# Last two down pairs in column parts of 308 and 220 with their weights kept on chip, and the last sums ahead of the spreads

## The chip, the core and the metric

The kernel runs on one NeuronCore of a Trainium2 chip. The metric is the device time of one execution in microseconds. The core has TensorE (matrix products into PSUM), VectorE, ScalarE, GpSimd and SyncE, which here only issues DMAs. The profile calls them PE (with PEld for the loading of weights), DVE, ACT, POOL and SP. All data is float32 in DRAM. Each engine runs its instructions in order, and semaphores are the only tie between engines.

## The reference

One layer of a decoder with three parallel token mixers, a gated merge, then a SwiGLU feed-forward and a final RMSNorm. The change touches the last part alone:

```python
h2 = rmsnorm(x, norm2_w)
gu = h2 @ w_ffn_up
x = x + ((silu(gu[..., :D_FF]) * gu[..., D_FF:]) @ w_ffn_down)
...
def rmsnorm(x, w):            # final norm, with final_norm_w
    return x * rsqrt(mean(x * x, axis=-1) + EPS) * w
```

with D_MODEL 1024, D_FF 2816 and 1056 tokens (1024 of the prompt, 32 of the samples). The outputs of the step are `y` for all tokens and the new states of the mixers.

## The kernel before, in words

The tensors lie with channels in the 128 partitions and the T = 1056 tokens along the free dimension. X1 holds the residual in 8 tiles of 128 channels (KD = 8). Each float32 operand of a large product is split into a high part (rounded to fp32r) and a low part, and a product is three matmuls (high weight by low data, low weight by high data, high by high), lines 2229 to 2231.

The feed-forward is done in *pairs*, each a 2 by 2 block product in Strassen's way: seven products, numbered 1 to 7, whose results are added to the four quadrants (two channel tiles by two halves of the 528 tokens). Pairs 0 to 19 are the up projection, pairs 20 to 35 (PAIRS = 36) the down projection: four groups of depth, with four pairs of output tiles in each. Pair 32 + m of the last group makes channel tiles 2m and 2m + 1 final, so pair 34 finishes tiles 4 and 5, pair 35 tiles 6 and 7. In this group a product is deep 3 tiles, so it is 3 x 3 matmuls for a *chunk* of columns. Each product covers 528 columns in two chunks of 264 (c = 0 and 1), in two PSUM banks (`quad`); one product is 18 matmuls.

**Weights.** For each product ScalarE casts the weight to its high part (`weight_high`, line 2762), and GpSimd subtracts to get the low part (`low`). Products 5, 7, 6 and 4 need a difference of raw weights first, made by GpSimd in place (`difference`). The order on GpSimd for a pair is: low of the first product, two differences, two lows, a difference, a low, a difference, three lows; all have line 1305. The parts go into a ring of six slots (`ring`), in WH, WL and RINGB. Slot g is free once product g - 6 is done, and ScalarE issues the cast of product g four products ahead (AHEAD). TensorE waits for the low part (`wl_ok`) ahead of each product. Raw weights are loaded two pairs ahead into RAWB (even pairs) and WRAW (odd pairs).

**Order of products.** Pairs take 1, 5, 7, 6, 2, 3, 4 (ORDER); the last pair takes 1, 5, 7, 6, 4, 3, 2 (LAST_ORDER) and is made chunk by chunk from its second product on: product 1 whole, six products for c = 0, six for c = 1. VectorE adds each result to X1 (`down_add`, `last_down_add`, line 2927), nine adds for a pair or a chunk of it, and product 6 enters three quadrants. A product may overwrite its bank only when the add of the bank's last product is done (semaphore `dd`).

**Final norm.** ScalarE squares each finished tile (into SQ5 and GT), VectorE adds the squares into AC5. Tiles 0 to 5 are added over all 1056 columns at once. Tiles 6 and 7 are done for four *groups* of 264 columns: group g is the upper half for g even, the lower for g odd, chunk g // 2. For a group TensorE sums AC5 over the partitions in three blocks of 88 tokens (`final_sums`, line 2259), ScalarE takes the root, VectorE the reciprocal, TensorE spreads it over the partitions (`final_spread`, line 2267), ScalarE copies it from PSUM (`spread_copy`). Then GpSimd scales tiles 0 to 2 and VectorE tiles 3 to 7 (`final_rows`, line 2935), and three DMAs store the group (tiles 0 to 2, 3 to 5, 6 and 7), all by SyncE but for the first of group 3, which ScalarE issues. Sums and spreads of groups 0 and 1 stand between products of the last chunk; those of groups 2 and 3 follow the last product as sums 2, spread 2, sums 3, spread 3. The order on each engine is written out by hand.

## Times and profile before

| | us |
|---|---|
| median of 3 executions | 1685.45 |
| lowest and highest | 1684.84, 1686.82 |
| profiled execution, its own time | 1684.72 |
| its span | 1683.0 |
| TensorE busy | 1653.4 (98%) |
| VectorE, ScalarE, GpSimd busy | 965.2, 556.0, 791.2 |

The span runs from the first instruction to the last of the profiled execution; the time of that execution is 1.7 us more. A matmul's busy time is longer than its distance to the next, since they are pipelined: its cost in a stream is the distance between starts. Times in the rows count from the start of the span. A row of the view in order of time has start, duration (of all that it merges), engine, line, operation, names written and read, shapes, how many, and in brackets the engine's idle time before it and what ended that. GpSimd and VectorE rows give the duration of a single instruction only where x1 stands.

### The profile page before, as it was taken

The numbers are of one execution on the slowest core, as the hardware profiler recorded it, in microseconds if no ns is written. First come the engines' busy times: TensorE is split into PE (matmuls) and PEld (weight loads), VectorE is DVE, ScalarE is ACT, GpSimd is POOL, SyncE is SP. The second block draws the span as 40 slices with busy tenths as digits, with TensorE's granted clock in tenths as the row PEclk, the third lists the DMA queues.
The fourth block names the chain that finished last, engine by engine and source line by source line (L and its number), as shares of the span: only waits on it lengthen the run. The fifth ranks groups of instructions, "written<-read, shape, count | busy, mean of one in ns | idle before, by whom it ended". The sixth has DMA issues, their size and how long they took to land. (4 is left out here: it accounts for less than half of the span.)

```text
span 1683.0 us, 30880 instructions
## 1 busy us (share of the span) xinstructions
PE 1653.4 (98%) x12241; PEld 1604.5 (95%) x12241; DVE 965.2 (57%) x1642; ACT 556.0 (33%) x1240; POOL 791.2 (47%) x756
## 2 busy tenths in 40 slices
PE   7999999999999999999999999999999999999997
PEld 7999999999999998889899999999999999999997
...
## 3 DMA queue, kind: packets, MB, share of 16 engines
...
q14 instruction: 42, 0.34, 0.1%
...
## 5 line engine op out<-in xcount | busy, mean ns | idle before, releaser
L1636 PE MATMUL ps<-HL,WH 128*128 128x384 f32 (+1 forms) x1536 | 507.3, 330 | 4.3 <-DVE HL L689 1.8
L1637 PE MATMUL ps<-HH,WL 128*128 128x384 f32 (+1 forms) x1536 | 496.9, 324 | 0.0
L1638 PE MATMUL ps<-HH,WH 128*128 128x384 f32 (+1 forms) x1536 | 496.1, 323 | 0.0
L1636 PEld LDWEIGHTS ps<-HL,WH 128*128 128x128 f32 x1536 | 289.2, 188 | 15.5 <-issue 9.4
L1637 PEld LDWEIGHTS ps<-HH,WL 128*128 128x128 f32 x1536 | 289.4, 188 | 0.3
L1638 PEld LDWEIGHTS ps<-HH,WH 128*128 128x128 f32 x1536 | 289.2, 188 | 0.0
L1280 POOL TENSOR_TENSOR WL<-WRAW,WH 128x1024 fp32r<-128x1024 f32 x59 | 145.6, 2467 | 246.9 <-DMA WH<-in_w 246.9
L1277 POOL DMA_DIRECT2D WH<-in_w x59 | 34.5, 585 | 348.6 <-PE ps L1638 347.1
L2927 DVE TENSOR_TENSOR X<-X,ps 128x528 f32<-128x528 f32 (+2 forms) x170 | 107.8, 655 | 155.3 <-PE ps L2231 104.4
L2320 ACT ACTIVATE GT<-ps 128x384 f32<-128x384 f32 (+1 forms) x72 | 33.3, 464 | 214.7 <-PE ps L1638 177.5
L2927 DVE TENSOR_TENSOR RB<-RB,ps 128x528 f32<-128x528 f32 x60 | 42.1, 701 | 103.5 <-ACT RB L2842 86.0
L1305 POOL TENSOR_TENSOR WRAW<-WRAW 128x512 f32<-128x512 f32 (+2 forms) x72 | 92.0, 1278 | 9.9 <-DVE STG L2927 4.6
L1305 POOL TENSOR_TENSOR RAWB<-RAWB 128x512 f32<-128x512 f32 (+2 forms) x72 | 87.5, 1215 | 5.4
L2229 PE MATMUL ps<-HL,RINGB 128*128 128x264 f32 x272 | 77.5, 285 | 2.1 <-DVE GT L2927 2.1
L2230 PE MATMUL ps<-HH,RINGB 128*128 128x264 f32 x280 | 79.5, 284 | 0.0
L2231 PE MATMUL ps<-HH,RINGB 128*128 128x264 f32 x280 | 79.5, 284 | 0.0
L2229 PE MATMUL ps<-HL,WH 128*128 128x264 f32 x274 | 78.0, 285 | 0.4 <-issue 0.4
L2229 PE MATMUL ps<-HL,WL 128*128 128x264 f32 x270 | 76.6, 284 | 0.0
L2229 PE MATMUL ps<-SOP,RINGB 128*128 128x264 f32 x264 | 75.2, 285 | 0.0
L2230 PE MATMUL ps<-HH,WL 128*128 128x264 f32 x264 | 75.0, 284 | 0.0
L2231 PE MATMUL ps<-SOP,RINGB 128*128 128x264 f32 x264 | 75.0, 284 | 0.0
L2230 PE MATMUL ps<-SOP,RINGB 128*128 128x264 f32 x264 | 74.9, 284 | 0.0
...
## 6 DMA issues: line engine op xcount, KB each, us to landing
...
```

Source lines behind the costliest of these rows:

```text
L1277: nc.gpsimd.dma_start(WH[:, slot, 0:wd], src[:, 0:wd]).then_inc(s_high[slot], 16)
L1280: nc.gpsimd.tensor_tensor(WL[:, slot, 0:wd], WRAW[:, slot, 0:wd], WH[:, slot, 0:wd].bitcast(F32), ALU.subtract).then_inc(split_ok, 1)
L1305: return nc.gpsimd.tensor_tensor(out, a, b, op)
L1636: nc.tensor.matmul(out, wh, rl, start=start, stop=False)
L1637: nc.tensor.matmul(out, wl, rh, start=False, stop=False)
L1638: return nc.tensor.matmul(out, wh, rh, start=False, stop=stop)
L2229: nc.tensor.matmul(out, wh, ml, start=product in FRESH and k == 0, stop=False, skip_group_check=True)
L2230: nc.tensor.matmul(out, wl, mh, start=False, stop=False, skip_group_check=True)
L2231: last = nc.tensor.matmul(out, wh, mh, start=False, stop=k == nk - 1, skip_group_check=True)
L2320: nc.scalar.activation(GT[:, c0:c0 + w], acc_of(no, n)[:, 0:w], ACT.Tanh, scale=0.5).then_inc(acc_free[n], 1)
L2927: return nc.vector.tensor_tensor(out, a, b, op)
```

## The change

Pairs 34 and 35 are both made in two parts. The first part covers columns 0 to 307 of each half, the second columns 308 to 527 (LAST_COLS). The order is: pair 34 first part (seven products of nine matmuls with 308 columns), pair 35 first part, pair 34 second part (220 columns), pair 35 second part. Both pairs use LAST_ORDER. The weights of product 2 of pair 34 and of all of pair 35 go to places of their own, in parts of HH, HL and SOP that the last group of depth doesn't use and in the new LASTB, so the six ring slots hold the other six products of pair 34, and all stay for both parts; their casts wait only for the end of pair 31. The groups have 308, 308, 220 and 220 columns, summed in four blocks of 77 tokens or two of 110. Squares of tiles 4 and 5 are made for both halves of a part by one instruction (`pair_square`). Sums 0 and 1, then spreads 0 and 1, stand in the second part of pair 34; after the last product come sums 2, sums 3, spread 2, spread 3. ScalarE now issues two stores of group 3.

On VectorE the adds of squares over 1056 columns (`AC<-`) stand at other places. Before, from the end of pair 33 on (X is the residual, ps a bank):

```order
L2927 TENSOR_TENSOR AC<-SQ,GT 128x1056
L2927 TENSOR_TENSOR X<-X,ps 128x528 x9
L2927 TENSOR_TENSOR AC<-AC,SQ 128x1056
L2927 TENSOR_TENSOR AC<-AC,GT 128x1056
L2927 TENSOR_TENSOR X<-X,ps 128x528 x4
L2927 TENSOR_TENSOR AC<-AC,SQ 128x1056
```

and with the change:

```order
L2965 TENSOR_TENSOR AC<-SQ,GT 128x1056
L2965 TENSOR_TENSOR X<-X,ps 128x528 x3
L2965 TENSOR_TENSOR X<-X,ps 128x308 x6
L2965 TENSOR_TENSOR AC<-AC,SQ 128x1056
L2965 TENSOR_TENSOR X<-X,ps 128x308 x4
L2965 TENSOR_TENSOR AC<-AC,GT 128x1056
L2965 TENSOR_TENSOR X<-X,ps 128x308 x5
L2965 TENSOR_TENSOR AC<-AC,GT 128x2x308
L2965 TENSOR_TENSOR AC<-AC,SQ 128x2x308
```

The two long adds that stood side by side within pair 34 now stand behind product 6 of pair 34 and behind product 1 of pair 35; a third is replaced by adds over both halves of one part.

On TensorE the end of the program was, from the last three matmuls of product 2 on (the sums read AC, the spreads RC):

```order
L2229 MATMUL ps<-HH,WL 128x264
L2230 MATMUL ps<-HH,WL 128x264
L2231 MATMUL ps<-HH,WL 128x264
L2259 MATMUL ps<-PRM,AC 88x1 x3
L2267 MATMUL ps<-PRM,RC 128x88 x3
L2259 MATMUL ps<-PRM,AC 88x1 x3
L2267 MATMUL ps<-PRM,RC 128x88 x3
```

and is now:

```order
L2257 MATMUL ps<-HH,SOP 128x220
L2258 MATMUL ps<-HH,LASTB 128x220
L2259 MATMUL ps<-HH,SOP 128x220
L2288 MATMUL ps<-PRM,AC 110x1 x4
L2296 MATMUL ps<-PRM,RC 128x110 x4
```

The sums of groups 2 and 3 (two blocks each) follow one another, and the two spreads come behind both.

```diff
@@ -69,8 +69,7 @@
 ORDER, LAST_ORDER = (1, 5, 7, 6, 2, 3, 4), (1, 5, 7, 6, 4, 3, 2)
 QUAD = {1: 0, 6: 0, 5: 2, 3: 2, 7: 4, 4: 4, 2: 6}
 FRESH = (1, 5, 7, 2)
-LAST_CHUNK = (5, 7, 6, 4, 3, 2)
-TOKENS = 88
+LAST_COLS = ((0, 308), (308, 220))
...
@@ -78,7 +77,7 @@
 
 def order_of(x):
 
-    return LAST_ORDER if x == PAIRS - 1 else ORDER
+    return LAST_ORDER if x >= PAIRS - 2 else ORDER
...
+
+    p5 = ExitStack()
+    sb(p5, "padLASTB", [P, 22 * T + 2 * 2048])
+    LASTB = sb(p5, "LASTB", [P, 384], F32R)
...
     BY_POOL = (0, 1, 2)
-    LAST = PAIRS - 1
+    FIRST_CUT, LAST = PAIRS - 2, PAIRS - 1
     GROUPS = 4
 
     def group_cols(g):
 
-        t0 = (HALF, 0)[g % 2] + CHUNK * (g // 2)
-        return slice(t0, t0 + CHUNK)
+        t0, w = LAST_COLS[g // 2]
+        t0 += (HALF, 0)[g % 2]
+        return slice(t0, t0 + w)
...
+
+    def both_halves(a, c):
+
+        t0, w = LAST_COLS[c]
+        return a.rearrange("p (h t) -> p h t", h=2)[:, :, t0:t0 + w]
...
@@ -904,6 +920,13 @@
     def ring(g):
 
         n = depth(g // 7) * P
+        e = g - 7 * FIRST_CUT - RING
+        if e >= 0:
+            spare = [t.rearrange("p a b -> p (a b)") for t in (HH[:, 2:4, :], HL[:, 6:8, :], SOP[:, 1:3, :])]
+            if e < 6:
+                part = spare[e // 2][:, 2 * n * (e % 2):2 * n * (e % 2) + 2 * n]
+                return part[:, 0:n], part[:, n:2 * n]
+            return ((spare[0][:, 4 * n:5 * n], spare[1][:, 4 * n:5 * n]), (spare[2][:, 4 * n:5 * n], LASTB[:, 0:n]))[e - 6]
...
@@ -951,6 +974,9 @@
     def quad(product):
         return ps_all[:, QUAD[product]:QUAD[product] + 2, 0:CHUNK]
 
+    def last_quad(product, c):
+        return bank[QUAD[product] + c][:, 0:LAST_COLS[c][1]]
...
@@ -974,6 +1000,8 @@
     def moving(x, product, k, c):
 
         cols = slice(CHUNK * c, CHUNK * c + CHUNK)
+        if x >= FIRST_CUT:
+            cols = slice(LAST_COLS[c][0], sum(LAST_COLS[c]))
...
@@ -1259,7 +1287,7 @@
                 f_load(d + 1, 6, done_count(x, ORDER[4]))
         for g in range(GROUPS):
             for rows in OUT_ROWS:
-                if (g, rows) != (GROUPS - 1, OUT_ROWS[0]):
+                if g < GROUPS - 1 or rows == OUT_ROWS[2]:
                     rows_done(sp, g, *rows)
                     sp.dma_start(*group_out(g, *rows)).then_inc(s_out, 16)
...
+        def last_product(x, c, product):
+
+            if (x, c) == (FIRST_CUT, 0):
+                bank_free(x, product)
+            else:
+                if product in (6, 4, 3):
+                    after(pe, dd, last_add(x, c, {6: 1, 4: 3, 3: 2}[product]))
+                if product in FRESH and x == LAST:
+                    after(pe, dd, last_add(FIRST_CUT, c, {1: 6, 5: 8, 7: 7, 2: 9}[product]))
+            i = LAST_ORDER.index(product)
             if c == 0:
-                after(pe, wl_ok, 7 * LAST + i + 1)
-            product_chunk(LAST, i, c).then_inc(pd.sem, 1)
+                after(pe, wl_ok, 7 * x + i + 1)
+            product_chunk(x, i, c).then_inc(pd.sem, 1)
...
-        for x in range(LAST):
+        for x in range(FIRST_CUT):
             for i in range(7):
                 strassen_product(x, i)
-        strassen_product(LAST, 0)
-        for product in LAST_CHUNK:
-            last_product(0, product)
-        last_product(1, 5)
-        final_sums(0)
-        last_product(1, 7)
-        final_spread(0)
-        final_sums(1)
-        last_product(1, 6)
-        final_spread(1)
-        for product in LAST_CHUNK[3:]:
-            last_product(1, product)
+        for x in (FIRST_CUT, LAST):
+            for product in LAST_ORDER:
+                last_product(x, 0, product)
+        for product in LAST_ORDER:
+            last_product(FIRST_CUT, 1, product)
+            if product == 5:
+                final_sums(0)
+            if product == 6:
+                final_sums(1)
+            if product == 4:
+                final_spread(0)
+            if product == 2:
+                final_spread(1)
+        for product in LAST_ORDER:
+            last_product(LAST, 1, product)
         final_sums(2)
+        final_sums(3)
         final_spread(2)
-        final_sums(3)
         final_spread(3)
...
-            if g >= RING:
+            if g >= 7 * FIRST_CUT + RING:
+                after(act, pd, 7 * (PAIRS - 4))
+            elif g >= RING:
                 after(act, pd, g - RING + 1)
...
-                if m >= 1 and i == 1:
+                if m in (1, 2) and i == 1:
                     if m >= 2:
-                        after(act, fad, (1, 3)[m - 2])
...
         def spread_copy(g):
...
+
+        def pair_square(k, c, out, adds):
+
+            after(act, dd, adds)
+            nc.scalar.activation(both_halves(out[:], c), both_halves(X1[:, k, :], c), ACT.Square).then_inc(fsq.sem, 1)
+
+        after(act, fad, 3)
         for c in range(2):
             u, l = group_cols(2 * c), group_cols(2 * c + 1)
-            final_square(7, u, GT, last_add(c, 3))
-            final_square(6, u, SQ5, last_add(c, 6))
-            final_square(7, l, GT, last_add(c, 7))
-            if c == 1:
-                final_root(2)
-            final_square(6, l, SQ5, last_add(c, 8))
-            if c == 0:
-                final_root(0)
-                spread_copy(0)
-                final_root(1)
-                spread_copy(1)
-        spread_copy(2)
-        final_root(3)
-        spread_copy(3)
-        rows_done(act, GROUPS - 1, *OUT_ROWS[0])
-        out_dma(*group_out(GROUPS - 1, *OUT_ROWS[0]))
-        assert outs[0] + 11 == N_OUT_TOTAL
+            pair_square(5, c, GT, last_add(FIRST_CUT, c, 8))
+            pair_square(4, c, SQ5, last_add(FIRST_CUT, c, 9))
+            after(act, fad, 4 + 6 * c)
+            final_square(7, u, GT, last_add(LAST, c, 4))
+            after(act, fad, 5 + 6 * c)
+            final_square(6, u, SQ5, last_add(LAST, c, 7))
+            final_square(7, l, GT, last_add(LAST, c, 8))
+            final_square(6, l, SQ5, last_add(LAST, c, 9))
+            final_root(2 * c)
+            final_root(2 * c + 1)
+            spread_copy(2 * c)
+            spread_copy(2 * c + 1)
+        for rows in OUT_ROWS[0:2]:
+            rows_done(act, GROUPS - 1, *rows)
+            out_dma(*group_out(GROUPS - 1, *rows))
...
+        def last_sixes(x, c):
+
+            last_down_add(x, c, 6, 1, 1, 3)
+            last_down_add(x, c, 6, 1, 0)
+            last_down_add(x, c, 6, 0, 1)
+
+        def pair_square_sum(k, c):
+
+            n = 5 + 6 * c + (k == 4)
+            after(dve, fsq, n)
+            after(dve, fad, n - 2)
+            a = both_halves(AC5[:], c)
+            tt(a, a, both_halves((SQ5, GT)[k - 4][:], c), ALU.add).then_inc(fad.sem, 1)
...
-            if d == 3 and m == 2:
-                for j in range(2):
-                    after(dve, fad, 1 + j)
-                    square_sum(slice(0, T), (SQ5, GT)[j], 3 + j)
...
-        down_add(LAST, 3, 0, 0, 1)
-        after(dve, fad, 3)
-        square_sum(slice(0, T), SQ5, 5)
-        last_down_add(0, 5, 1, 1)
-        last_down_add(0, 7, 1, 1, 1)
-        last_down_add(0, 6, 1, 1, 2)
-        last_down_add(0, 6, 1, 0)
-        last_down_add(0, 6, 0, 1)
-        after(dve, fad, 4)
-        square_sum(slice(0, T), GT, 6)
-        after(dve, fad, 5)
+        A = FIRST_CUT
+        last_down_add(A, 0, 1, 0, 0)
+        last_down_add(A, 0, 5, 1, 1)
+        last_down_add(A, 0, 7, 1, 1, 2)
+        last_sixes(A, 0)
+        after(dve, fad, 1)
+        square_sum(slice(0, T), SQ5, 3)
+        last_down_add(A, 0, 4, 1, 0, 5)
+        last_down_add(A, 0, 3, 0, 1, 6)
+        last_down_add(A, 0, 2, 0, 0, 1)
+        last_down_add(LAST, 0, 1, 0, 0)
+        after(dve, fad, 2)
+        square_sum(slice(0, T), GT, 4)
+        last_down_add(LAST, 0, 5, 1, 1)
+        last_down_add(LAST, 0, 7, 1, 1, 2)
+        last_sixes(LAST, 0)
+        pair_square_sum(5, 0)
+        pair_square_sum(4, 0)
         group_square_sum(0, 7)
-        last_down_add(0, 4, 1, 0, 4)
-        last_down_add(0, 3, 0, 1, 5)
+        last_down_add(LAST, 0, 4, 1, 0, 5)
+        last_down_add(LAST, 0, 3, 0, 1, 6)
         group_square_sum(0, 6)
-        last_down_add(0, 2, 0, 0, 0)
+        last_down_add(LAST, 0, 2, 0, 0, 1)
         group_square_sum(1, 7)
+        last_down_add(A, 1, 1, 0, 0)
         group_square_sum(1, 6)
+        last_down_add(A, 1, 5, 1, 1)
+        last_down_add(A, 1, 7, 1, 1, 2)
         final_recip(0)
-        last_down_add(1, 5, 1, 1)
+        last_sixes(A, 1)
+        final_recip(1)
+        last_down_add(A, 1, 4, 1, 0, 5)
+        last_down_add(A, 1, 3, 0, 1, 6)
         final_rows(0, (3, 4))
-        final_recip(1)
-        final_rows(0, (5,))
-        last_down_add(1, 7, 1, 1, 1)
-        final_rows(0, (6, 7))
-        final_rows(1, (3, 4))
-        last_down_add(1, 6, 1, 1, 2)
-        last_down_add(1, 6, 1, 0)
-        last_down_add(1, 6, 0, 1)
+        last_down_add(A, 1, 2, 0, 0, 1)
+        final_rows(0, (5, 6))
+        last_down_add(LAST, 1, 1, 0, 0)
+        final_rows(0, (7,))
+        last_down_add(LAST, 1, 5, 1, 1)
+        pair_square_sum(5, 1)
+        last_down_add(LAST, 1, 7, 1, 1, 2)
+        pair_square_sum(4, 1)
+        last_sixes(LAST, 1)
+        final_rows(1, (3,))
         group_square_sum(2, 7)
-        last_down_add(1, 4, 1, 0, 4)
-        last_down_add(1, 3, 0, 1, 5)
+        last_down_add(LAST, 1, 4, 1, 0, 5)
+        final_rows(1, (4,))
+        last_down_add(LAST, 1, 3, 0, 1, 6)
         group_square_sum(2, 6)
-        last_down_add(1, 2, 0, 0)
+        last_down_add(LAST, 1, 2, 0, 0, 1)
         group_square_sum(3, 7)
+        final_rows(1, (5,))
+        group_square_sum(3, 6)
         final_recip(2)
-        group_square_sum(3, 6)
-        final_rows(1, (5, 6, 7))
-        final_rows(2, (3, 4))
+        final_rows(1, (6, 7))
         final_recip(3)
-        final_rows(2, (5, 6, 7))
+        final_rows(2, range(3, KD))
         final_rows(3, range(3, KD))
```

## Rows read from the trace of the kernel before

**Rows 1.** Busy time by stretches: us, then each engine, PEclk, DMA share, GB/s:
```profile
1634.50:1649.90 15.40, 15.40 (x128) 15.40 (x128) 9.29 (x11) 6.03 (x9) 13.15 (x12) 1.00 0.01 2
1668.30:1683.00 14.70, 4.19 (x24) 3.79 (x24) 7.34 (x20) 2.31 (x7) 4.28 (x6) 0.59 0.72 244
```

**Rows 2.** TensorE in order of time (start, us, ...), first matmuls of pairs 34, 35:
```profile
1634.43 0.28 PE L2229 MATMUL ps<-HH,WL 128*128 128x264 f32 x1
...
1649.78 0.28 PE L2229 MATMUL ps<-HH,WL 128*128 128x264 f32 x1
```

**Rows 3.** TensorE in order of time, around 406 us, matmuls of other widths:
```profile
399.67 0.34 PE L1637 MATMUL ps<-HH,WL 128*128 128x384 f32 x1
...
405.82 0.29 PE L1636 MATMUL ps<-HL,WH 128*128 128x288 f32 x1
...
407.94 0.29 PE L1637 MATMUL ps<-HH,WL 128*128 128x288 f32 x1
```

**Rows 4.** TensorE in order of time, 78 to 80 us, matmuls of 32 columns:
```profile
77.96 0.41 PE L1787 MATMUL ps<-CDG,W_re 128*128 128x32 f32 x2
...
79.54 0.39 PE L1787 MATMUL ps<-CDG,W_im 128*128 128x32 f32 x2
```

**Rows 5.** GpSimd in order of time, 1634 to 1652 us:
```profile
1634.49 1.02 POOL L1305 TENSOR_TENSOR RAWB<-RAWB 128x384 f32<-128x384 f32 x1
1635.46 2.00 POOL L1305 TENSOR_TENSOR WH<-RAWB,WH 128x384 fp32r<-128x384 f32 x2
1637.97 1.02 POOL L1305 TENSOR_TENSOR WL<-RAWB,WL 128x384 fp32r<-128x384 f32 x1 [0.51 <-ACT WL L2762]
1639.66 1.01 POOL L1305 TENSOR_TENSOR WL<-WRAW,WL 128x384 fp32r<-128x384 f32 x1 [0.67 <-ACT WL L2762]
1640.75 2.17 POOL L1305 TENSOR_TENSOR WRAW<-WRAW 128x384 f32<-128x384 f32 x2
1642.89 2.12 POOL L1305 TENSOR_TENSOR RINGB<-WRAW,RINGB 128x384 fp32r<-128x384 f32 x2
1644.97 1.02 POOL L1305 TENSOR_TENSOR WRAW<-WRAW 128x384 f32<-128x384 f32 x1
1646.68 1.29 POOL L1305 TENSOR_TENSOR WH<-WRAW,WH 128x384 fp32r<-128x384 f32 x1 [0.70 <-ACT WH L2762]
1648.05 1.92 POOL L1305 TENSOR_TENSOR WRAW<-WRAW 128x384 f32<-128x384 f32 x1
1650.67 1.03 POOL L1305 TENSOR_TENSOR WH<-WRAW,WH 128x384 fp32r<-128x384 f32 x1 [0.70 <-ACT WH L2762]
```

**Rows 6.** VectorE in order of time, its adds of 1056 columns:
```profile
1645.24 1.85 DVE L2927 TENSOR_TENSOR AC<-AC,SQ 128x1056 f32<-128x1056 f32 x1
1647.13 1.95 DVE L2927 TENSOR_TENSOR AC<-AC,GT 128x1056 f32<-128x1056 f32 x1
...
1652.78 1.25 DVE L2927 TENSOR_TENSOR AC<-AC,SQ 128x1056 f32<-128x1056 f32 x1
```

**Rows 7.** ScalarE in order of time, the cast for product 4 of pair 35:
```profile
1650.08 0.51 ACT L2762 CAST WH<-WRAW 128x384 fp32r<-128x384 f32 x1 [3.47 <-POOL WRAW L1305]
```

**Rows 8.** TensorE in order of time, first sums and last product:
```profile
1659.49 0.28 PE L2231 MATMUL ps<-SOP,RINGB 128*128 128x264 f32 x1
1660.09 0.63 PE L2259 MATMUL ps<-PRM,AC 128*88 128x1 f32 x6 [0.33 <-DVE AC L2927]
...
1668.01 0.29 PE L2231 MATMUL ps<-HH,WL 128*128 128x264 f32 x1
```

**Rows 9.** GpSimd in order of time, rows of groups 2 and 3:
```profile
1672.20 2.14 POOL L1305 TENSOR_TENSOR X<-X,SPREAD 128x264 f32<-128x264 f32 x3 [4.60 <-ACT SPREAD L2890]
1675.27 2.14 POOL L1305 TENSOR_TENSOR X<-X,SPREAD 128x264 f32<-128x264 f32 x3 [0.92 <-ACT SPREAD L2890]
```

**Rows 10.** Busy time by stretches around the last stores:
```profile
1674.50:1675.20 0.70, 0.28 (x2) 0.05 (x1) 0.00 (x0) 0.38 (x1) 0.00 (x0) 0.50 0.00 0
1675.30:1681.50 6.20, 0.00 (x0) 0.00 (x0) 2.01 (x5) 0.00 (x0) 2.11 (x3) 0.50 1.02 346
```

68 lines of the change are left out of this document (33 added, 35 removed).

## The prediction

> **What bounds the kernel now.** I read the busy table by stretches first, then TensorE in order of time, then GpSimd, VectorE and ScalarE over the same stretch, and last the end of the kernel with the DMA share. In pair 34, the second last, TensorE works all 15.4 us at full clock [rows 1]; there a microsecond counts if TensorE does it or waits for it. After its last product (start 1668.01 [rows 8]) comes a tail of 14.7 us [rows 1] that is a chain: the last squares, sums, root, spread, copy, scaling of rows, stores. GpSimd is the engine to watch ahead of that: it is busy 13.15 of the 15.40 us [rows 1], making the down weights. Before, that is covered, since a pair lasts 15.35 us. The change makes the first part of the two pairs shorter than that, so the cover has to be worked out again.
>
> **Term 1, column widths.** With 264 columns 126 matmuls take 1649.78 - 1634.43 = 15.35 us, 0.1218 us each (0.1215 in runs without a break) [rows 2]. With 384 columns it is 35 in 6.15 us, 0.1757 each; with 288 it is 16 in 2.12 us, 0.1325 [rows 3]. All three are 0.458 to 0.461 ns a column, so 308 columns cost 0.141 us. For 220 this line gives 0.101. But each matmul also loads 128 columns of weights, and matmuls of only 32 columns with such weights still take (79.54 - 77.96)/14 = 0.113 us [rows 4]. So 220 columns cost between 0.101 (no floor) and 0.1215 (as 264); I take 0.112, the floor of the nearest row. 126 matmuls at 308: +0.0197 x 126 = +2.5 us. 126 at 220: -0.0095 x 126 = -1.2 us (ends -2.6 and 0). Sum **+1.3 us**, between -0.1 and +2.5.
>
> The Trainium skill (TensorE: Matmul & The Clock Gate, LDWEIGHTS) gives a weight load as its columns divided by 1.2 GHz, 107 ns for 128 columns; by that figure the second part would cost -1.8 and the term would be an estimated +0.7 us. The row's 113 ns agrees with the rule but for 6 ns.
>
> **Term 2, sums and spreads inside the stream.** Between the starts 1659.49 and 1668.01 stand 45 product matmuls (5.47 us), so two sum and two spread blocks with their waits cost 3.05 us, some 0.5 of it the wait of the first sums (1660.09 against 1659.61) [rows 8]. Groups 0 and 1 now have four blocks of 77 tokens, not three of 88: 8/6 of 2.55 is 3.4, less some tenths for narrower weights. The wait goes: VectorE adds the last square of group 0 behind the sixth product of pair 35, three products ahead of the sums. **+0.2 us** (0 to 0.5).
>
> **Term 3, the supply of weights.** Pairs 34 and 35 in their first part take 9 x 0.141 = 1.27 us a product, 8.9 us a pair, where the weights of a pair were spread over 15.35. GpSimd does 11 instructions for a pair (four differences, seven low parts) at 1.0 to 1.08 us each [rows 5], and low parts of products 5, 7, 6, 4 wait for difference, then cast by ScalarE, then subtract: 0.7 us idle each time [rows 5]. Neither ring slots nor anything else gated product 4 of pair 35 before: ScalarE waited 3.47 us for GpSimd's difference there [rows 7], and the low part ended at 1650.67 + 1.03 = 1651.70 [rows 5]. The new slots remove only the wait for a free slot before the first low part of pair 35 (in the 0.67 us of 1639.66 [rows 5]).
>
> Three things push the chain back. First, pair 34 takes the order of the last pair, so its fifth product is 4, whose cast must wait for the difference of 1634.49 + 1.02; two casts and the two squares behind them come 1 us later, the low part for product 2 at about 1639.0 instead of 1637.97, the first of pair 35 at 1640.0 (before 1639.66). Second, a VectorE add of two 1056-column tensors in SBUF and a GpSimd instruction exclude each other: the GpSimd instructions that began at 1646.68 and 1648.05 ran inside such adds (1645.24 + 1.85 = 1647.09; 1647.13 + 1.95 = 1649.08) [rows 6] and ended 0.88 and 0.89 us after these, in 1.29 and 1.92 us instead of 1.0 [rows 5]; the adds themselves took 1.85 and 1.95 where one with GpSimd idle took 1.25 [rows 6]. Third, these adds now come earlier, at some 1640.8 (behind product 6 of pair 34) and 1645.2 (behind product 1 of pair 35). The first catches the difference for product 5 (ready 1643.0, before 1641.8), the second the low part of product 7.
>
> The Trainium skill (SBUF — State Buffer, SBUF: two separate sides) says the same of this pair: whoever starts first holds the shared port for its whole instruction and the other blocks, also for two SBUF inputs on VectorE. The two ends at +0.88 agree with it; by that rule the supply costs the 4.3 us below, and if the longer times had another cause, 1.2.
>
> Followed with these durations, pair 35's weights are ready, against the start TensorE would like (1634.43 + 8.89, then + 1.27 each):
> product 1: 1641.0, wanted 1643.3; product 5: 1645.2, wanted 1644.6; product 7: 1647.3, wanted 1645.9; product 6: 1650.0, wanted 1647.1; product 4: 1652.7, wanted 1648.4; products 3 and 2 one GpSimd instruction (1.0 us) apart each, faster than TensorE takes them. Lateness does not add: the stretch ends 1652.7 - 1648.4 = **+4.3 us** late, in four idle stretches of 0.6 to 1.4 us. The chain's end of 1652.7 is only 1.0 later than before's 1651.70, while the demand is much earlier. Lower end: without the exclusion GpSimd would have product 4 ready near 1649.6, 1.2 us late. Upper end: one more collision, 5.3.
>
> I see no other wait on TensorE: the tightest bank wait, product 4 on product 7's add, has a whole product of 1.0 us or more between them against an add of under 0.5; the others have more, and in the second part all weights are there.
>
> **Term 4, the tail.** Before: last matmul out at 1668.29; GpSimd scales group 2 from 1672.20 to 1674.34 and group 3 until 1677.41 [rows 9]; the DMA engines are idle from 1674.5 to 1675.2 and then full from 1675.3 for 6.2 us [rows 10], for groups 2 and 3 (2.16 MB); another 1.5 us to the end. What ends last is these two groups through the DMA engines, from the moment group 2 is scaled (+6.05 us after the last product). Now: VectorE's last add, square, add of the square 1.4 us; sums of both groups and the spread of group 2 by 2.55; copy 2.95; three rows of GpSimd at 0.713 x 220/264 = 0.6 us: 4.8; first bytes 0.95 later as before (1675.3 - 1674.34): 5.7; 1.80 MB at the same rate 5.2; end 1.5. That is 12.4 against 14.7: **-2.3 us** (-1.6 to -3.0). The spreads of group 3 may run at the clock of 1.2 GHz, which the tail reached before (mean 0.59 over its 14.7 us, 0.50 at its end, so full for its first 2.6 us) [rows 1, 10]; group 3 is hidden behind GpSimd's rows of group 2. Stores of groups 0 and 1, 1.26 MB each, are over by then.
>
> **Sum.** +1.3 + 0.2 + 4.3 - 2.3 = +3.5 us. The profiled execution took 1684.72 us (span 1683.0), so 1688.2; it lies 0.7 under the median of 1685.45, from which the same sum gives 1688.95. I predict **1688.5 us**. A difference under 0.2%, 3.4 us, can't be told from none in this kernel, and the forecast sits on that line.
>
> **Rivals.**
> A. The weights come in time, or nearly: the exclusion costs pair 35 nothing, because VectorE's adds fall into GpSimd's waits for ScalarE. For it: an exclusion costs only where starts fall inside. Against: GpSimd then has few gaps. The stall is 1.2 us or less: 1.3 + 0.2 + 1.2 - 2.3 = +0.4, 1685.5 us. Chance 0.15.
> B. Faster than before: no floor under 220 columns, no stall, and a tail at its best, -0.1 + 0 + 0 - 3.0 = -3.1 us, 1682 us. It decides from the point where product 4's weights are ready by 1648.4; rows show 1651.70 before, with GpSimd the reason. Chance 0.06, and past 0.2% faster 0.03.
> C. The clock: TensorE works little more than half the time between 1644.6 and 1653, and its clock falls to 1.2 GHz there as it did 2.6 us after the last product before. Matmuls of 308 columns would take up to twice as long; the wait for weights covers most in products 5 to 6, not in 4, 3 and 2 (3 x 1.27 us): +2 to +4 on top, 1691.5 us. Against: the products keep coming, with no gap over 1.5 us. Chance 0.12.
> D. 220 columns as dear as 264: +1.2 on top, 1689.7 us. Chance 0.12.
> The forecast itself, with 1686.5 to 1690, has 0.55.
>
> **How the numbers follow.** Past +3.4 us lie half of the forecast (0.28), C and most of D: 0.50. Past 0.2% faster 0.03, rounded to 0.04; the rest, 0.46, is no difference that can be told. The range takes in A at the lower end and C at the upper: 1684.9 to 1692.0; the forecast's own range is 1686.5 to 1690.
>
> **What would show it.** TensorE idle ahead of products 5, 7, 6 and 4 of pair 35's first part, released by GpSimd's low parts, some 4.3 us in all (Term 3; none, and A or B holds). Spacing of the 220-column matmuls near 0.112 us (0.101: no floor; 0.12: D), of those with 308 near 0.141. GpSimd instructions of 1.3 us and more beside VectorE's 1056-column adds. From the last product to the end 12.4 us, with the DMA engines full over the last two groups. A granted clock under 1.00 between 1640 and 1660 would be C. The forecast is wrong as a whole if the last product starts less than 3 or more than 8 us later than 1668.01.

## The result, and the profile after

The changed kernel takes **1689.61 us** (median of 15 executions, 1687.85 to 1693.01), the kernel before 1686.10 in the 15 run beside it: ratio 1.0020, 95% interval 1.0013 to 1.0027, slower by 3.5 us. The forecast was 1688.5, from a sum of +3.5 us. The profiled execution of the changed kernel took 1693.01 us, its span 1691.3, against 1684.72 and 1683.0: 8.3 us more, over twice the difference of the medians, so it has to be cut up before it is read.

The stretches of the changed kernel (columns as in [rows 1]): three early ones, the first part of pair 35, and the tail.

```profile
386.40:389.70 3.30, 3.30 (x12) 3.30 (x11) 1.98 (x2) 0.80 (x3) 1.84 (x1) 0.50 0.45 119
768.70:772.00 3.30, 3.30 (x12) 3.30 (x11) 3.12 (x4) 0.00 (x0) 2.10 (x1) 0.50 0.76 221
1052.00:1055.30 3.30, 3.30 (x17) 3.30 (x17) 3.00 (x4) 2.07 (x4) 3.30 (x3) 0.50 0.91 258
...
1647.90:1656.30 8.40, 4.82 (x29) 3.91 (x29) 3.82 (x7) 2.85 (x7) 6.87 (x7) 0.99 0.00 0
1656.30:1659.50 3.20, 3.19 (x12) 3.20 (x13) 1.35 (x3) 2.79 (x5) 1.81 (x2) 0.50 0.00 0
1678.90:1691.30 12.40, 2.33 (x16) 1.89 (x16) 6.19 (x19) 1.75 (x6) 3.69 (x6) 0.68 0.64 209
```

The first three rows lie in work that the change does not touch: there TensorE ran at 1.2 GHz, and pair 34 began at 1637.84 instead of 1634.43 [rows 2]. Other profiled executions below have none, one or two such stretches and begin pair 34 between 1634.2 and 1636.9. So 3.4 of the 8.3 us arose before the change begins, and from here on I count from pair 34's first matmul. In the first part of pair 35 TensorE is busy 4.82 of 8.40 us; then it works at half clock, 1.2 GHz (the row shows 3.2 of some 3.4 us).

TensorE in order of time in that stretch (first matmuls of products 5, 7, 6, 4 of pair 35), then the first 220-column matmul and the end; a bracket gives the idle time ahead:

```profile
1637.84 0.30 PE L2257 MATMUL ps<-HH,WL 128*128 128x308 f32 x1
...
1648.70 0.38 PE L2257 MATMUL ps<-HH,HL 128*128 128x308 f32 x1 [0.52 <-DVE X L2965]
...
1650.87 0.38 PE L2257 MATMUL ps<-HH,HL 128*128 128x308 f32 x1 [0.65 <-DVE X L2965]
...
1653.52 0.38 PE L2257 MATMUL ps<-SOP 128*128 128x308 f32 x1 [1.14 <-POOL SOP L1333]
...
1656.31 0.60 PE L2257 MATMUL ps<-HL,SOP 128*128 128x308 f32 x1 [1.27 <-POOL SOP L1333]
1656.70 0.46 PE L2258 MATMUL ps<-HL,SOP 128*128 128x308 f32 x1
...
1661.66 0.27 PE L2257 MATMUL ps<-HH,WL 128*128 128x220 f32 x1
...
1678.58 0.27 PE L2259 MATMUL ps<-HH,SOP 128*128 128x220 f32 x1
1679.06 0.55 PE L2288 MATMUL ps<-PRM,AC 128*110 128x1 f32 x4 [0.21 <-DVE AC L2965]
1680.42 0.55 PE L2288 MATMUL ps<-PRM,AC 128*110 128x1 f32 x4 [0.81 <-DVE AC L2965]
1680.83 1.39 PE L2296 MATMUL ps<-PRM,RC 110*128 110x110 f32 x8
```

Four idle stretches, as forecast. The view puts the first two down to VectorE, but the adds that these products wait for had ended by 1646.3; GpSimd's rows say what released them. GpSimd in order of time, and VectorE's two long adds (they answer to [rows 5, 6]):

```profile
1643.37 1.02 POOL L1333 TENSOR_TENSOR HH<-WRAW,HH 128x384 fp32r<-128x384 f32 x1
1644.46 1.96 POOL L1333 TENSOR_TENSOR WRAW<-WRAW 128x384 f32<-128x384 f32 x1
...
1646.57 1.02 POOL L1333 TENSOR_TENSOR WRAW<-WRAW 128x384 f32<-128x384 f32 x1
1647.54 1.01 POOL L1333 TENSOR_TENSOR HL<-WRAW,HL 128x384 fp32r<-128x384 f32 x1
...
1648.61 2.12 POOL L1333 TENSOR_TENSOR HL<-WRAW,HL 128x384 fp32r<-128x384 f32 x1
1650.68 0.99 POOL L1333 TENSOR_TENSOR WRAW<-WRAW 128x384 f32<-128x384 f32 x1
1652.38 1.00 POOL L1333 TENSOR_TENSOR SOP<-WRAW,SOP 128x384 fp32r<-128x384 f32 x1 [0.70 <-ACT SOP L2796]
1653.46 1.01 POOL L1333 TENSOR_TENSOR WRAW<-WRAW 128x384 f32<-128x384 f32 x1
1655.16 1.00 POOL L1333 TENSOR_TENSOR SOP<-WRAW,SOP 128x384 fp32r<-128x384 f32 x1 [0.70 <-ACT SOP L2796]
```
```profile
1644.29 1.25 DVE L2965 TENSOR_TENSOR AC<-AC,SQ 128x1056 f32<-128x1056 f32 x1
...
1648.61 1.25 DVE L2965 TENSOR_TENSOR AC<-AC,GT 128x1056 f32<-128x1056 f32 x1
```

The low parts of products 5, 7, 6 and 4 end at 1648.55, 1650.73, 1653.38 and 1656.16, and each product starts 0.14 to 0.15 us later. The two GpSimd instructions that began inside a long add or with it took 1.96 and 2.12 us, their neighbours 1.0; both ended 0.87 to 0.88 us after the add.

Cut at these rows, against the kernel before:

| part | before | after | difference |
|---|---|---|---|
| 251 distances between product matmuls (308 columns: 0.1413, 220: 0.1119, 264: 0.1215 us) | 30.5 | 31.8 | +1.3 |
| sums and spreads inside the stream | 3.1 | 2.9 | -0.1 |
| late weights: product 4 starts at 1656.31 where 99 matmuls at 0.1413 end at 1651.83 | 0 | 4.5 | +4.5 |
| 1.2 GHz in pair 35: 5.35 us for 27 matmuls that need 3.8 | 0 | 1.5 | +1.5 |
| start of the last matmul to the end of the span | 15.0 | 12.7 | -2.3 |
| from pair 34's start | 48.6 | 53.5 | +4.9 |

Without the half-clock stretch it is +3.4 us (52.0 us from pair 34's start), which is what the medians show. The fastest executions differ by as much: 1687.85, at a mean granted clock of 0.998 (0.994 in the profiled execution), against 1684.54.

The stretches around the stores answer to [rows 10]: from 1678 to 1681 nothing moves, group 1's last rows go till 1683.3, groups 2 and 3 fill the DMA engines for 5.5 us instead of 6.2.

```profile
1678.00:1681.00 3.00, 1.98 (x17) 1.72 (x17) 3.00 (x10) 1.35 (x4) 0.00 (x0) 1.00 0.00 0
1681.00:1683.30 2.30, 1.20 (x8) 0.84 (x7) 1.85 (x6) 0.95 (x3) 1.34 (x3) 1.00 0.98 339
1684.80:1690.30 5.50, 0.00 (x0) 0.00 (x0) 0.74 (x3) 0.00 (x0) 0.84 (x2) 0.50 1.03 326
```

### The profile page after: what moved, and what is told of

It reads as the page before. It is cut to its first block and busy times, and to the rows that moved or that the text cites. A ratio compares the mean times of both kernels' runs of the same rounds, so it can differ in the third digit from the quotient of the medians.

```text
span 1691.3 us, 30909 instructions
## 1 busy us (share of the span) xinstructions
PE 1659.6 (98%) x12241; PEld 1609.9 (95%) x12241; DVE 964.9 (57%) x1654; ACT 555.9 (33%) x1242; POOL 791.3 (47%) x756
## 5 line engine op out<-in xcount | busy, mean ns | idle before, releaser
L2965 DVE TENSOR_TENSOR X<-X,ps 128x528 f32<-128x528 f32 (+3 forms) x180 | 109.5, 628 | 161.1 <-PE ps L2259 110.0
L2258 PE MATMUL ps<-HH,RINGB 128*128 128x264 f32 (+1 forms) x276 | 79.1, 287 | 0.0
L2259 PE MATMUL ps<-HH,RINGB 128*128 128x264 f32 (+1 forms) x276 | 79.1, 287 | 0.0
L2257 PE MATMUL ps<-HL,WH 128*128 128x264 f32 (+1 forms) x270 | 76.9, 285 | 0.3 <-issue 0.3
L2257 PE MATMUL ps<-HL,WL 128*128 128x264 f32 x258 | 73.2, 284 | 0.0
L2257 PE MATMUL ps<-SOP,RINGB 128*128 128x264 f32 (+2 forms) x256 | 72.9, 285 | 0.1
L1333 POOL TENSOR_TENSOR RINGB<-RAWB,RINGB 128x512 fp32r<-128x512 f32 (+2 forms) x42 | 52.0, 1240 | 44.4 <-ACT RINGB L2796 44.4
L2258 PE MATMUL ps<-HH,WL 128*128 128x264 f32 (+1 forms) x256 | 72.8, 284 | 0.0
L2259 PE MATMUL ps<-SOP,RINGB 128*128 128x264 f32 (+2 forms) x256 | 72.7, 284 | 0.0
```

The source lines that it names most:

```text
L1333: return nc.gpsimd.tensor_tensor(out, a, b, op)
L2257: nc.tensor.matmul(out, wh, ml, start=product in FRESH and k == 0, stop=False, skip_group_check=True)
L2258: nc.tensor.matmul(out, wl, mh, start=False, stop=False, skip_group_check=True)
L2259: last = nc.tensor.matmul(out, wh, mh, start=False, stop=k == nk - 1, skip_group_check=True)
L2965: return nc.vector.tensor_tensor(out, a, b, op)
```

## The experiments

Every kernel was timed 11 times (the changed one 15, e1 6, e12 12) beside the kernel before on the same chip (the experiments ran on four chips), whose medians there were 1686.0 to 1686.7 us; the ratio is to these. 0.001 of ratio is 1.7 us. "Stream" runs from pair 34's first matmul to the start of the last product's last matmul, "tail" from there to the end of the span, both in the one profiled execution; "low" is time at 1.2 GHz inside the stream. The gain or loss of a kernel is its ratio; stream and tail say where it is. For the size of a step, the changed kernel's sum is best taken without its 1.5 us of half clock, as 52.0.

| kernel | median us | ratio to before, 95% | stream | low | tail | sum |
|---|---|---|---|---|---|---|
| before | 1686.10 | 1 | 33.57 | 0 | 14.99 | 48.6 |
| changed | 1689.61 | 1.0020 (1.0013 to 1.0027) | 40.74 | 3.4 | 12.72 | 53.5 |
| e1 long adds late | 1695.57 | 1.0044 (1.0027 to 1.0061) | 44.82 | 10.2 | 12.72 | 57.5 |
| e2 squares late | 1687.19 | 1.0004 (0.9996 to 1.0013) | 36.65 | 0 | 12.74 | 49.4 |
| e3 264 and 264 | 1690.79 | 1.0026 (1.0017 to 1.0035) | 39.12 | 3.4 | 14.11 | 53.2 |
| e4 last pair alone | 1687.50 | 1.0005 (0.9996 to 1.0013) | 34.71 | 0 | 14.69 | 49.4 |
| e5 tail's order alone | 1687.26 | 1.0003 (0.9994 to 1.0012) | 33.57 | 0 | 15.91 | 49.5 |
| e6 short differences | 1689.08 | 1.0014 (1.0005 to 1.0023) | 37.35 | 0 | 13.25 | 50.6 |
| e7 last pair alone, rows moved | 1686.81 | 0.9999 (0.9990 to 1.0008) | 34.81 | 0 | 13.61 | 48.4 |
| e8 e2, one add moved | 1686.34 | 0.9998 (0.9989 to 1.0008) | 35.90 | 0 | 12.77 | 48.7 |
| e9 e2, both adds moved | 1685.36 | 0.9995 (0.9986 to 1.0004) | 35.18 | 0 | 13.30 | 48.5 |
| e10 e9, old tail order | 1685.04 | 0.9993 (0.9984 to 1.0002) | 35.19 | 0 | 12.84 | 48.0 |
| e11 e9 with 330 and 198 | 1686.10 | 1.0000 (0.9991 to 1.0009) | 36.31 | 0 | 12.44 | 48.8 |
| e12 e10, reciprocal earlier | 1684.07 | 0.9991 (0.9983 to 1.0000) | 35.15 | 0 | 12.14 | 47.3 |

**e1, the long adds late.**

```diff
         last_sixes(A, 0)
-        after(dve, fad, 1)
-        square_sum(slice(0, T), SQ5, 3)
...
-        after(dve, fad, 2)
-        square_sum(slice(0, T), GT, 4)
         last_down_add(LAST, 0, 5, 1, 1)
         last_down_add(LAST, 0, 7, 1, 1, 2)
         last_sixes(LAST, 0)
+        after(dve, fad, 1)
+        square_sum(slice(0, T), SQ5, 3)
+        after(dve, fad, 2)
+        square_sum(slice(0, T), GT, 4)
```

> The changed kernel, but VectorE makes its two adds of 1056 columns (for the sums of rows 3 and 4) behind the sixth product's corrections of the last pair instead of between them, so that they no longer stand over GpSimd's splits of the weights. Theory (the weights of the last pair come too late: the splits on GpSimd, two of them made three times as dear by a VectorE add, leave four idle stretches of about 4.3 us in all ahead of products 5, 7, 6 and 4 of the last pair's first part): GpSimd's splits of 3.1 us fall to about 1.0, the idle stretches ahead of 5, 7, 6 and 4 fall to some 2.7 us, but the first column sums, which read those adds, now wait some 2 us in the stream of products; in all 0 to +0.8 us against the changed kernel, 1689.6 to 1690.4. Rival (the four idle stretches are not VectorE's doing, ScalarE's casts alone set them): they stay at 4.3 us and the sums wait on top, 1691.5. Rival (the two collisions are all that makes the weights late, and the sums have room): 1687.5.

TensorE's waits in e1, its stretches from the first sums on, and GpSimd's low parts of products 1 and 4 of pair 35:

```profile
1650.50 0.38 PE L2257 MATMUL ps<-SOP 128*128 128x308 f32 x1 [0.75 <-POOL SOP L1333]
1653.30 0.38 PE L2257 MATMUL ps<-HL,SOP 128*128 128x308 f32 x1 [1.29 <-DVE X L2965]
1656.26 0.38 PE L2257 MATMUL ps<-HL,SOP 128*128 128x308 f32 x1 [0.17 <-POOL LASTB L1333]
...
1661.81 0.71 PE L2288 MATMUL ps<-PRM,AC 128*77 128x1 f32 x8 [2.03 <-DVE AC L2965]
```
```profile
1663.10:1673.30 10.20, 10.20 (x53) 10.20 (x53) 3.09 (x11) 0.68 (x2) 2.17 (x3) 0.50 0.01 2
1673.40:1681.80 8.40, 8.40 (x77) 8.37 (x75) 7.45 (x20) 2.12 (x5) 2.65 (x4) 1.00 0.59 207
```
```profile
1642.38 1.02 POOL L1333 TENSOR_TENSOR HH<-WRAW,HH 128x384 fp32r<-128x384 f32 x1
...
1652.15 1.00 POOL L1333 TENSOR_TENSOR SOP<-WRAW,SOP 128x384 fp32r<-128x384 f32 x1 [0.70 <-ACT SOP L2796]
```

The waits are as the theory said: of the four idle stretches those ahead of 5 and 7 are gone, 2.0 us stand in front of the sums instead. ("Three times as dear" was a misreading of a row that merges two instructions; singly they take 2.0 to 2.1 us, twice as long.) GpSimd's chain, from the end of the low part of product 1 to that of product 4, takes 9.75 us instead of 11.77: the two meetings with the long adds are worth 2.0 us of supply. The time is not as expected: behind the wait for the sums TensorE ran at half clock for 10.2 us, though it was busy all of it. From the first matmul behind sums 0 to the first behind spread 1 it took 12.27 us (1662.39 to 1674.66) where the changed kernel took 7.40, so 4.9 us dearer. Two of the six executions took 1689.8 and 1690.5, as expected; the other four 1695.0 to 1697.9. I take those four for executions with this stretch, since the profiled one, 1696.1, is among them; that is not shown, the others were not profiled.

**e2, ScalarE's squares of pair 34 two casts later** (and its products by the norm's weights, those in pair 33 too).

```diff
-                if m in (1, 2) and i == 1:
+                if m in (1, 2) and i == (1, 3)[m - 1]:
...
-                if m in (1, 2) and i == 4:
+                if m in (1, 2) and i == 6:
```

> The changed kernel, but ScalarE makes the two squares of pair 34's rows (and the two products by the norm's weights behind them) two casts of weights later in its list. Theory (supply of the weights): the casts for products 5, 7, 6 and 4 of the last pair come some 3 us earlier, GpSimd's splits follow them, the idle stretches fall from 4.3 us to about 1.5, and the time falls by 2 to 2.8 us, to 1687.0 (1686.6 to 1687.6). Rival (the gain was lost in the widths of 308 and 220 columns and the idle stretches are hidden by something else that comes just behind): within 0.5 us of the changed kernel, 1689.6. Rival (GpSimd itself is the bound there and ScalarE's order is nothing): idle stretches unchanged, 1689.6.

ScalarE in the changed kernel (two squares, then the cast for product 1 of pair 35); then e2, TensorE ahead of product 4 and GpSimd's low parts of products 1 and 4:

```profile
1639.86 1.08 ACT L2896 ACTIVATE SQ<-X 128x1056 f32<-128x1056 f32 x1
1640.85 1.06 ACT L2896 ACTIVATE GT<-X 128x1056 f32<-128x1056 f32 x1
...
1642.22 0.51 ACT L2796 CAST HH<-WRAW 128x384 fp32r<-128x384 f32 x1
```

```profile
1651.93 0.38 PE L2257 MATMUL ps<-HL,SOP 128*128 128x308 f32 x1 [1.28 <-DVE X L2965]
```
```profile
1639.04 1.03 POOL L1333 TENSOR_TENSOR HH<-WRAW,HH 128x384 fp32r<-128x384 f32 x1
...
1650.79 1.00 POOL L1333 TENSOR_TENSOR SOP<-WRAW,SOP 128x384 fp32r<-128x384 f32 x1 [0.70 <-ACT SOP L2796]
```

As the theory said: one idle stretch of 1.28 us is left, ahead of product 4, the clock stays up, and the median is 1687.19. The ratio falls by 0.0016, some 2.7 us. The chain itself is as long as in the changed kernel (11.72 against 11.77 us), both meetings with the long adds are still in it; but it begins 3.96 us behind pair 34's start (1636.11) instead of 6.55. So the casts queued behind two squares of 1.08 us each are the larger of the two causes, 2.6 us against 2.0.

**e3, equal parts.**

```diff
-LAST_COLS = ((0, 308), (308, 220))
+LAST_COLS = ((0, 264), (264, 264))
...
-        return (77, 110)[g // 2]
+        return (88, 88)[g // 2]
```

> The changed kernel with parts of 264 and 264 columns per half instead of 308 and 220. Theory (Term 1 of the prediction, widths cost 1.3 us because 220 columns take 112 ns, 0.51 per column, where 308 take 0.459; Term 3, idle stretches): the widths' 1.3 us come back, but the first part of the last pair takes 72 x 20 ns less per part, so the weights are wanted earlier and the idle stretches grow by about 1.5 us; the tail behind the last product grows by 0.5 to 1 us with the wider last part. In all +0.8 to +2 us, 1691.0. Rival (unequal widths are the whole of the loss): 1688.0 or less. Rival (as dear as the changed kernel, all three cancel): 1689.6.

By ratio +1.0 us over the changed kernel, with intervals that overlap; the sum, 53.2 against 52.0, says +1.2. The trace shows both sides of it, TensorE's waits first:

```profile
1646.14 0.36 PE L2257 MATMUL ps<-HH,HL 128*128 128x264 f32 x1 [2.87 <-POOL HL L1333]
...
1652.55 0.36 PE L2257 MATMUL ps<-HL,SOP 128*128 128x264 f32 x1 [1.02 <-POOL SOP L1333]
```

Weights are wanted earlier and waited for longer, and the tail is 1.4 us longer than with 220 columns. The unequal widths are not the loss.

**e4, the last pair alone in 308 and 220** (pair 34 whole, tail in the new order). Its first product stands in other columns than those added to it in PSUM, so its last rows of y are not the reference's; instructions and sizes are those of the comparison.

```diff
+        if x == LAST and product != 1:
+            cols = slice(LAST_COLS[c][0], sum(LAST_COLS[c]))
...
         final_sums(2)
-        final_spread(2)
         final_sums(3)
+        final_spread(2)
         final_spread(3)
```

> The kernel before, with its last pair alone in parts of 308 and 220 columns (its first product still whole, pair 34 in one part with weights used once for each product), and with the last sums ahead of the spreads. It is the change without the two-part pair 34. Theory (pair 34's parts and the late weights cost all of the loss, the tail gains): no idle stretch ahead of products 5, 7, 6, 4; widths cost about 0.6 us, a tail of about 13 us behind the last product instead of 14.7 gives back 1.0 to 1.7 us; in all -0.2 (-1.2 to +0.3) against the kernel before, 1685.9. Rival (narrow last part costs more than its tail gives back): +1, 1687.1. Rival (the tail gives its full 2.3 us here): 1684.4.

No idle stretch ahead of pair 35's products, and the stream 1.1 us longer. But the tail is 14.69 us, where the theory had 13: VectorE scales rows of groups 0 and 1, now 308 columns wide, ahead of the additions that the last sums wait for. By ratio +0.8 us: nearer to the rival's +1 than to the theory's -0.2, though the interval (-0.7 to +2.2) holds both.

**e5, the tail's order alone**, in the kernel before (ScalarE's and VectorE's lists follow).

```diff
         final_sums(2)
-        final_spread(2)
         final_sums(3)
+        final_spread(2)
         final_spread(3)
```

> The kernel before with one edit: behind the last product TensorE makes both column sums (groups 2 and 3) ahead of both spreads, and ScalarE's roots, copies and VectorE's reciprocals follow that order. Theory A (the tail of the changed kernel, 12.5 us against 14.7 behind the last product, came from the narrow last part of 220 columns and from VectorE's lighter load in the second part, not from the order): the order alone gives nothing or costs up to 0.5 us, since group 2's spread comes later and its rows and stores with it; 1686.4 to 1687.2. Rival B (the order gives the tail's gain): the tail falls by 1 us or more, 1685.5 or less.

The tail grows from 14.99 to 15.91 us, the time by 0.5 us by ratio (interval across one). "Last sums ahead of spreads" gains nothing by itself: group 2's spread starts 3.5 us behind the last matmul's start instead of 2.5 (1672.70 - 1669.19 against 1670.47 - 1668.01), and its rows and stores with it.

**e6, the last pair's differences over 32 of 128 columns** (the weights of four products are then not the reference's).

```diff
+            c = 32 if x == LAST else P
-            tt(raw_part(x, *out), raw_part(x, *a), raw_part(x, *b), ALU.subtract).then_inc(wt_ok.sem, 1)
+            tt(raw_part(x, *out)[:, :, 0:c], raw_part(x, *a)[:, :, 0:c], raw_part(x, *b)[:, :, 0:c], ALU.subtract).then_inc(wt_ok.sem, 1)
```

> The changed kernel, but GpSimd forms the four differences of the last pair's weights over 32 of each 128 columns alone (the weights of products 5, 7, 6 and 4 are then not the reference's). Theory (the chain difference, cast, split on GpSimd and ScalarE sets when the last pair's products can start): the idle stretches ahead of products 5 and 7 go, those ahead of 6 and 4 shrink to about 2 us together, and 2 to 2.6 us of 4.3 come back, 1687.3. Rival (the idle stretches come from another wait, the free weight slots or PSUM banks): they stay, 1689.6.

The idle stretches went as said: none ahead of 5 and 7, 1.45 and 0.66 us ahead of 6 and 4. The time did not: product 4 starts 2.0 us earlier behind pair 34's start, yet the sum falls only by 1.4, from 52.0 to 50.6, since the tail is 0.5 longer, and the ratio says 1.0 where 2 to 2.6 was expected. The clock may account for the tail: it fell 2.2 us behind the last matmul's start here, 4.8 in the changed kernel. The intervals of the two kernels overlap, so 2 us is not excluded either.

**e7, the last pair alone, its first product in the same widths**, the old order of the tail, and two rows of group 1 behind the additions.

```diff
-        final_rows(1, (3, 4))
         last_down_add(1, 6, 1, 1, 2)
...
         last_down_add(1, 3, 0, 1, 5)
+        final_rows(1, (3,))
         group_square_sum(2, 6)
         last_down_add(1, 2, 0, 0)
         group_square_sum(3, 7)
+        final_rows(1, (4,))
```

> The kernel before (pair 34 whole, last sums in their old order) with its last pair, the first product too, in parts of 308 and 220 columns, and VectorE's two rows 3 and 4 of group 1 made behind the additions for group 2's sums instead of ahead of them. Theory (what gained in the change is the narrow last part, what lost was pair 34 in two parts with the late weights of pair 35): no idle stretch ahead of pair 35's products, widths cost 0.7 us, the tail behind the last product is about 13 us instead of 14.7; in all -1.1 us (-2.0 to 0) against the kernel before, 1685.5, and faster than both kernels. Rival (e4's layout, +0.8 us over the kernel before, shows that widths cost more than the tail gives): +0.5 to +1, 1687.3.

Tail 13.61 us, 1.4 less than before, stream +1.24: a wash in this execution. By ratio -0.2 us (-1.7 to +1.3): no gain is shown, and the expected -1.1 is not excluded. The tail is shorter than the 14.69 of e4, which has the rows ahead of the additions and the other order of sums. The stream cost 1.24 us where I had put 0.7 for the widths.

**e8, e9: VectorE's long adds.** e8 is e2 with the second add behind product 5's; e9 moves the first one too.

```diff
-        after(dve, fad, 1)
-        square_sum(slice(0, T), SQ5, 3)
         last_down_add(A, 0, 4, 1, 0, 5)
         last_down_add(A, 0, 3, 0, 1, 6)
+        after(dve, fad, 1)
+        square_sum(slice(0, T), SQ5, 3)
         last_down_add(A, 0, 2, 0, 0, 1)
         last_down_add(LAST, 0, 1, 0, 0)
-        after(dve, fad, 2)
-        square_sum(slice(0, T), GT, 4)
         last_down_add(LAST, 0, 5, 1, 1)
+        after(dve, fad, 2)
+        square_sum(slice(0, T), GT, 4)
```

> The kernel of the late squares (ScalarE makes pair 34's squares two casts later) with VectorE's second add of 1056 columns moved behind the add for product 5 of the last pair, so that it stands over a difference instead of over the split for product 6. Theory (GpSimd's chain sets the one idle stretch that was left, 1.3 us ahead of product 4, and the add that stands over the split makes it 1.0 us dearer): the idle stretch falls to about 0.8 us or less, 0.3 to 0.8 us come back, 1686.6. Rival (an add over a difference costs as much as one over a split): 1687.2, idle stretch unchanged.

> The changed kernel with ScalarE's squares of pair 34 two casts later, VectorE's second add of 1056 columns behind the add for product 5 of the last pair, and its first add of 1056 columns behind the add for product 3 of pair 34, where GpSimd is in a difference with a wait behind it. Theory (all of the change's idle stretches come from ScalarE's order and from VectorE's two long adds standing over GpSimd's splits): the one idle stretch that was left (0.9 us ahead of product 4) falls to 0.2 to 0.4 us; from pair 34's start to the end of the span 48.0 us (47.7 to 48.6) against 53.5 of the changed kernel and 48.6 of the kernel before; 1685.8, a little under the kernel before. Rival (the long add costs GpSimd 1 us wherever it stands): 48.7 us and 1686.4, as in the run with the second add alone moved.

The idle stretch ahead of product 4 goes from 1.28 (e2) to 0.90 (e8) to 0.17 us (e9), the stream from 36.65 to 35.90 to 35.18, and GpSimd's chain takes 11.72, 10.96 and 10.24 us. By ratio that is -1.0 us for e8 against e2, where 0.3 to 0.8 was expected, and -0.5 for e9 against e8; neither step is clear of the intervals by itself. In e9 a long add still meets GpSimd, but starts second (GpSimd, then VectorE, then TensorE ahead of product 4):

```profile
1642.33 1.02 POOL L1333 TENSOR_TENSOR WRAW<-WRAW 128x384 f32<-128x384 f32 x1
1644.05 1.29 POOL L1333 TENSOR_TENSOR SOP<-WRAW,SOP 128x384 fp32r<-128x384 f32 x1 [0.70 <-ACT SOP L2796]
```
```profile
1642.44 2.03 DVE L2965 TENSOR_TENSOR AC<-AC,SQ 128x1056 f32<-128x1056 f32 x1
...
1646.27 1.28 DVE L2965 TENSOR_TENSOR AC<-AC,GT 128x1056 f32<-128x1056 f32 x1
```
```profile
1648.57 0.38 PE L2257 MATMUL ps<-HL,SOP 128*128 128x308 f32 x1 [0.17 <-POOL SOP L1333]
```

The add that began at 1642.44, inside a difference, waited for it (2.03 instead of 1.25 us) and ran while GpSimd waited for ScalarE's cast; GpSimd lost 0.27 us, not 1. The second add began at 1646.27, 0.16 us before the end of a difference, and cost the low part behind it as little. Where the add comes, not that it comes, is what costs. The tail of 13.30 in e9's execution has TensorE at half clock from 1671.6, 2.2 us behind the last matmul's start, as early as in e6 (tail 13.25); in e2 and e8, with the same end of the program, it was 3.4 and 5.0 us (tails 12.74 and 12.77). The eight spreads took 2.03 us for it, 1.39 in those two.

**e10, e12: the old order of the tail on top of e9**; e12 has the last reciprocal one row earlier.

```diff
         final_sums(2)
-        final_sums(3)
         final_spread(2)
+        final_sums(3)
         final_spread(3)
```

> The same kernel, but with the last sums and spreads in the order of the kernel before: sums of group 2, its spread, sums of group 3, its spread, with ScalarE's roots and VectorE's reciprocals in that order. Theory (the new order costs: in the kernel before it made the tail 0.9 us longer): the tail from the last product's last matmul falls from 12.75 us by 0.3 to 0.9, and this is the fastest of all, 1685.2. Rival (in the two-part layout the order pays, since VectorE gets both sums' squares done one behind the other): the tail grows by 0.3 to 1 us, 1686.5.

> The fastest kernel so far (supply of weights mended, last sums and spreads in the old order) with VectorE's last reciprocal one row earlier. Theory: group 3's spread starts 0.3 us earlier, but the stores fill the DMA engines from the moment group 2's rows are there, so that at most 0.3 us of it reaches the end; -1.5 us (-2.5 to -0.5) against the kernel before, 1685.0, as the run of the same kernel without that edit: this is above all its second measurement. Rival (its lead over the kernel before was chance): within 0.5 us of the kernel before, 1686.3.

Both are faster than the changed kernel (intervals apart from its own) and 1.2 and 1.5 us under the kernel before by ratio; e12's interval ends at 1.0000. A gain over the kernel before of about 1.5 us is likely, not shown beyond doubt. What the order alone is worth, 0.3 us of medians between e9 and e10, can't be told from none, and the tail did not fall from 12.75 us as expected (12.84). In e12 it is 0.7 us shorter than in e10, but there the clock fell 5.3 us behind the last matmul's start, in e10 3.9, so the reciprocal's part is not separated.

**e11, 330 and 198 columns.**

```diff
-LAST_COLS = ((0, 308), (308, 220))
+LAST_COLS = ((0, 330), (330, 198))
...
-        return (77, 110)[g // 2]
+        return (110, 66)[g // 2]
```

> The kernel with the supply mended (new tail order) with parts of 330 and 198 columns instead of 308 and 220. Theory (a matmul of few columns takes 112 ns whatever its width, one of many 0.459 ns per column): 198 columns take 112 ns as 220 do, 330 take 151.5 instead of 141.3; product time +1.3 us over both pairs, less 0.2 to 0.4 of idle that it covers, tail -0.5 us; in all +0.1 to +0.8 against the 308 and 220 of the same call. Rival (198 columns are cheaper than 220, 0.51 per column: 101 ns): product time 0 and a gain of 0.8 us or more.

Neighbouring matmuls of 198 columns stand as far apart as those of 220 (first and last of nine, TensorE in order of time):

```profile
1654.28 0.27 PE L2259 MATMUL ps<-HH,WL 128*128 128x198 f32 x1
...
1655.17 0.27 PE L2258 MATMUL ps<-HH,WL 128*128 128x198 f32 x1
```

8 spacings in 0.89 us, 0.111 each; those of 330 take 0.151. The stream is 1.1 us longer than e9's, and the median 0.7, as expected: a floor of 0.111 to 0.112 us shows at 198 columns as at 220.

## Why the prediction was right

The sum said +3.5 us, the medians say +3.5 and the parts without the half clock +3.4. The chosen 1688.5 was lower than the sum on the median, and the kernel before ran 0.65 us slower beside the changed one than in its first three executions; hence 1.1 us between 1688.5 and 1689.61. One sign of being wrong as a whole came up: the last product's last matmul starts 10.6 us later than 1668.01, beyond the 8 that I allowed. That sign counted from the start of the span; from pair 34's start it is 7.2 us, 1.5 of them half clock.

**Term 1, widths, +1.3: right.** 0.1413 and 0.1119 us a matmul, forecast 0.141 and 0.112; e11 shows the floor under 220 as well. The Trainium skill (TensorE: Matmul & The Clock Gate, LDWEIGHTS) has 107 ns for 128 columns of weights; the spacings of 198 and 220 agree with it but for 4 to 5 ns. Rival D is out.

**Term 2, sums and spreads, +0.2: measured -0.1.** The first sums' wait went, as said; the narrower blocks cost less than I gave them.

**Term 3, supply, +4.3: measured +4.5.** Counted from pair 34's start, products 5, 7, 6 and 4 began at 1645.3, 1647.5, 1650.1 and 1652.9, against 1645.2, 1647.3, 1650.0 and 1652.7 forecast. e2, e8 and e9 take it away step by step (stream 40.7, 36.7, 35.9, 35.2 us). The total was right; its split was not. The mechanism has two parts that simply add up. One is where GpSimd's chain for pair 35 begins, the other how long it is up to product 4:

| kernel | low part of product 1 ends behind pair 34's start | from there to the low part of product 4 | product 4 late by |
|---|---|---|---|
| changed | 6.55 | 11.77 | 4.5 |
| e1 long adds late | 6.54 | 9.75 | 2.5 |
| e2 squares late | 3.96 | 11.72 | 1.8 |
| e8 | 3.97 | 10.96 | 1.1 |
| e9 | 3.96 | 10.24 | 0.4 |

The forecast's 1641.0 for the begin of the chain and 1652.7 for its end are these 6.55 and 11.77 to 0.1 us. What failed was the lower end, product 4's weights at 1649.6 and 1.2 us late without the exclusion. Eight GpSimd instructions of 1.0 to 1.08 us and two waits of 0.7 behind 1641.0 come to some 1650.7, and e1 measures it: 2.5 us late. So the exclusion is worth 2.0 us, not the 3.1 between 4.3 and 1.2, and rival A was priced 1.1 us too low. The 2.6 us of the squares ahead of the casts lay in the begin of the chain, where I never asked what they cost. That the starts agree does not tell such parts apart; only taking them away did. The Trainium skill (SBUF — State Buffer, SBUF: two separate sides) says that whoever starts first keeps the other out; e9's rows agree (2.03 us for the add that started second, 1.02 for the difference that started first). The description of the chip above calls semaphores the only tie between the engines; this exclusion is a second one.

**Term 4, tail, 12.4: measured 12.45** from the last product's end. That it fits so well is in part luck: first bytes of groups 2 and 3 at 5.9 us (forecast 5.7), 5.5 us of full DMA engines (5.2), and 1.0 to the end (1.5) cancel. Of the gain of 2.3 us the narrow last part makes 1.4 (e3 with 264); the rest may be VectorE's lists, which no run varies alone. The order of sums and spreads, which the change names, gains nothing (e5).

**Rival C, the clock**, came true in the profiled execution, at 1.5 us instead of the 2 to 4 that I gave it, and at the place named. My argument against it was weak: no gap was over 1.5 us, as I said (0.5 to 1.3), and the clock fell all the same. The medians sum up without it (+3.4 of +3.5), so the typical loss needs none of it; how often it comes is open, since one execution alone was profiled. Rivals A and B are out.
